# Prompt attention with the values stationary and two heads in column halves, the inverse softmax sums applied later by GpSimd

## The chip, the cores and the metric

The kernel runs on one core of a Trainium2 chip. It is written for the single engines: TensorE (PE, matmuls), VectorE (DVE), ScalarE (ACT), GpSimd (POOL) and SyncE (SP, whose queue issues nearly all DMAs). They run side by side and wait for each other on semaphores. The metric is the device time of one execution in microseconds (us).

## The reference, cut to what matters

One layer of a hybrid decoder is computed for a prompt of 256 positions and for 8 sequences of one new token with 2048 cached positions each: a macaron FFN, a combined projection, latent attention (MLA) beside a convolution branch, a gated merge, and a second FFN. The change lies in the attention of the prompt (16 heads, head width 96 for queries and keys, 64 for values):

```python
s = jnp.einsum('bqhd,bkhd->bhqk', qb, k) * scale
s = jnp.where(k_pos[None, :] <= qp[:, None], s, -jnp.inf)
p = jax.nn.softmax(s, axis=-1)
return jnp.einsum('bhqk,bkhd->bqhd', p, v)
# ... and behind it
a_out = jnp.einsum('bthd,hdo->bto', o, wts['w_attn_out'])
```

## The kernel before, in words

All is written out by hand, one program for each engine, so the order of work on an engine is the order of the code. The stages are: FFN 1, the projections, the prompt heads, the decode rounds (8 sequences of 16 cache pages of 128 positions), the gate stage, the attention output, convolution output and merge products, FFN 2. Products that need more than one pass are three matmuls of fp32r halves (L1894 to L1896, in `product`); the prompt attention, the transposes and the small products are plain fp32 matmuls.

**Prompt heads.** Two query tiles of 128 are kept as rows of scores: the first tile meets 128 keys, the second 256, so a head has 384 score columns. For each head PE makes the scores (L2287, L2288) into one of two PSUM banks. DVE adds the causal mask and puts the result into SBUF as `sS` (L1581), then takes two negated maxima `nm` (L1584, L1585). ACT takes the exponentials into `pS` with their sums `ls` (L1010, L1011). PE turns `pS` with three transposes (`turn_probs`, L2308), ACT copies them to `pTs` (`turned`, L1003), and PE multiplies (`values`): the probabilities are the stationary operand with 128 columns, the values move with 64 columns, three matmuls a head (L2320, L2322, L2323). Every four heads DVE takes reciprocals of the sums (L1593) and scales the result into `otok`, which has query positions on the partitions (`heads_out`, L1596). Scores of head n+2 are issued ahead of the transposes of head n. After the first three score pairs PE also makes one block of the conditioning product (`mod_rows`, L1971). Near the end of the heads PE turns the convolution state of the decode sequences (`turn_state`, L2297, two blocks of eight transposes) and ACT copies it to `stbuf` (L996).

**Decode rounds.** `sequence` goes through 16 pages. For a page PE transposes the cached latent (`turn`, L2342, L2343), ACT and DVE split it into `kTH` (L1026) and `kTL` (L1609), PE makes 18 matmuls with `wqH`, `wqL` (`keys`), ACT squares (L1038), DVE sums (L1614) and puts taps of the convolution between (L1701). At page 10 of the following sequence PE makes the weighted latents (`page_values`, L2367, stationary operands of 32 columns in four strips of the array). At page 6 ACT makes the probabilities (`p_done`) and GpSimd copies one row block of them (L679). SP loads the pages of sequence b+2 when PE has released their slots (`sample_pages`, L418 to L428).

**Gate stage.** Between the gate products PE transposes `otok` back, four transposes for each pair of 128-column blocks (`turn_heads`, L2426), and ACT copies them to `oT` (L1087), from which `oH` and `oL` are split for the attention output product.

Of the kernel before, what the change touches and what calls it, by code (L numbers as in the profile page):

```python
# [87 lines left out]
GATE_BANKS = (2, 6, 4, 6, 4, 6, 4, 6)  # L88

# [49 lines left out]
def decoder_layer(nc, x, out):  # L139
    ctx = ExitStack()  # L140
    with ctx:
# [88 lines left out]
        otok = sb("otok", [P, 2, H, VH], at=o)  # L230
# [18 lines left out]
        sS = sb("sS", [P, 2, 384], at=o + 8192)  # L249
        pS = sb("pS", [P, 2, 384], at=o + 11264)  # L250
        qtokS = qtok[:, 2, 0:H // 4, :]
        pTs = sb("pTs", [P, 2, 384], at=o + 14336)
        zst = sb("zst", [CW - 1 + NB, D], at=X + 14208)
        ctmp = sb("ctmp", [P, 2, T], at=o)
        kTH = sb("kTH", [P, 2, KL], F32R, at=o)
# [5 lines left out]
        oT = sb("oT", [P, KT, T], at=o + 8448)  # L261
# [3 lines left out]
        olrow = sb("olrow", [P, NB // 2, KL], at=o)  # L265
        S = sb("S", [P, 2, NPG + 1, H], at=o + 4096)
# [10 lines left out]
        qrT = sb("qrT", [P, H, NB], at=o); o += 512 + 928  # L277
# [7 lines left out]
        nm = sb("nm", [P, 2, 2], at=o); o += 32  # L285
# [15 lines left out]
        SCORES = [(0, 0), (2, 320)]  # L301

# [57 lines left out]
        ot_ps, ot_sb = sem("ot_ps"), sem("ot_sb")  # L360
# [29 lines left out]
        def _(sp):  # L390
# [226 lines left out]
        def _(pool):  # L617
# [19 lines left out]
            pool.wait_ge(pv_ps, H)  # L637
            nc.gpsimd.memset(Pr[:, :, :, :], 0.0)
            nc.gpsimd.memset(S[:, :, NPG, :], NEG).then_inc(memz, 1)

# [27 lines left out]
            sample_rows(0)  # L668
            for b in range(NB):
# [36 lines left out]
        def _(act):  # L706
# [285 lines left out]
            def state_columns(i):  # L992

                act.wait_ge(st_ps, i + 1)
                for n in range(2):
                    f(stbuf[:, 4 * n:4 * n + 4, 4 * i:4 * i + 4, :].rearrange("p f b t -> p f (b t)"),  # L996
                      PS[:, 6 + n, 0:480].rearrange("p (f c) -> p f c", f=4), ACT.Copy).then_inc(st_sb, 1)

            def turned(hd):
                act.wait_ge(pT_ps, hd + 1)  # L1000
                if hd >= 2:
                    act.wait_ge(pv_ps, hd - 1)
                f(pTs[:, hd % 2, :], PS[:, 2 + hd % 2, 0:384], ACT.Copy).then_inc(pT_sb, 1)  # L1003

            for hd in range(H):
                s = hd % 2
# [4 lines left out]
                f(pS[:, s, 128:384], sS[:, s, 128:384], ACT.Exp, bias=nm[:, s, 1:2], accum_out=ls[:, 1, hd:hd + 1]  # L1011
                  ).then_inc(exp_done, 1)
                if hd >= 1:
                    turned(hd - 1)
                if hd == 15:
                    state_columns(0)
            turned(H - 1)

            def page_hi(pg, n):
                act.wait_ge(kT_ps, pg + 1)
                act.wait_ge(kn_ps, pg + 1)
                if n % 4 == 0:
                    f(krT[:, (n // 4) % 2, :], PS[:, 0, KL:KL + P], ACT.Copy)
                f(kTH[:, n % 2, :], PS[:, 0, 0:KL], ACT.Copy).then_inc(kTH_done, 1)  # L1026
# [25 lines left out]
            def sequence(b, s, first=False, last=False):  # L1052
                for n in range(NPG):
                    pg = NPG * b + n
                    if not (last and n == NPG - 1):
                        page_hi(pg + 1, (n + 1) % NPG)
                    if n == 1 and not first:
                        norm_roots(b - 1, 1 - s)
# [7 lines left out]
            page_hi(0, 0)  # L1066
            state_columns(1)
            act.wait_ge(memz, 6)
# [13 lines left out]
            def heads_turned(i):  # L1082

                act.wait_ge(ot_ps, i + 1)
                if i == 0:
                    act.wait_ge(knsum_done, PAGES + 2)
                f(oT[:, 2 * i:2 * i + 2, 0:SEQ], PS[:, (4, 5, 2, 3)[i], :].rearrange("p (k n) -> p k n", k=2), ACT.Copy  # L1087
                  ).then_inc(ot_sb, 1)

            gate_columns(0)  # L1090
            heads_turned(0)
            heads_turned(1)
            gate_columns(1)
            gate_columns(2)
            heads_turned(2)
            heads_turned(3)
            act.wait_ge(ot_sb, 4)
            act.wait_ge(ysum_done, NB)
            for kt in range(KT):
                f(oH[:, kt, 0:SEQ], oT[:, kt, 0:SEQ], ACT.Copy).then_inc(oh_done, 1)  # L1100
# [5 lines left out]
            act.wait_ge(ot_ps, 5)  # L1106
# [55 lines left out]
        def _(dve):  # L1162
# [412 lines left out]

            def mask_max(hd):
                s = hd % 2
                dve.wait_ge(sc_ps, hd + 1)
                if hd >= 2:
                    dve.wait_ge(exp_done, hd - 1)  # L1580
# [3 lines left out]
                v.tensor_reduce(nm[:, s, 0:1], sS[:, s, 0:128], AX_X, ALU.max, negate=True)  # L1584
# [303 lines left out]
        def _(pe):  # L1888
# [390 lines left out]
            def scores(hd):  # L2279
# [3 lines left out]
                if hd == 1:  # L2283
                    pe.wait_ge(rest_sb, 5)
# [249 lines left out]
```

## Time and profile before

| | us |
|---|---|
| Median of three runs | 1142.21 (1141.67 to 1143.9) |
| The profiled execution, its own time | 1142.67 |
| Its span in the profile | 1140.8 |
| PE busy | 1122.6 (98%) |
| DVE busy | 779.2 (68%) |
| ACT busy | 581.7 (51%) |
| GpSimd busy | 66.9 (6%) |
| Mean granted TensorE clock | 0.997 of full |

The span is the time from the first to the last instruction of the profiled execution; 1.9 us of its own time lie around it. Busy times overlap, so only the engine on which the chain of waits lies sets the end. The chain is given in pieces "start, duration, what"; it counts a matmul from the end of the one before it, so its start times stand some 0.1 to 0.2 us behind those of the timeline for the same instruction. "x2" is the number of instructions in a piece; a plain fp32 matmul shows as two, a transpose as one.

### The profile page before, as it was taken

The numbers are of one execution on the slowest core, as the hardware profiler recorded it, in microseconds if no ns is written. First come the engines' busy times: TensorE is split into PE (matmuls) and PEld (weight loads), VectorE is DVE, ScalarE is ACT, GpSimd is POOL, SyncE is SP. The second block draws the span as 40 slices with busy tenths as digits, with TensorE's granted clock in tenths as the row PEclk, the third lists the DMA queues.
The fourth block names the chain that finished last, engine by engine and source line by source line (L and its number), as shares of the span: only waits on it lengthen the run. The fifth ranks groups of instructions, "written<-read, shape, count | busy, mean of one in ns | idle before, by whom it ended". The sixth has DMA issues, their size and how long they took to land.

```text
span 1140.8 us, 25908 instructions
## 1 busy us (share of the span) xinstructions
PE 1122.6 (98%) x9549; PEld 1087.0 (95%) x9549; DVE 779.2 (68%) x1325; ACT 581.7 (51%) x1153; POOL 66.9 (6%) x136
## 2 busy tenths in 40 slices
PE   5999999999999999999999999999999999999998
PEld 3999999999898999999999999999999999999998
DVE  4655553467777688888888888888756666555543
ACT  3444453346576655554545454554566445444432
POOL 2000000010000100101010110101020010000000
PEclk9899999999999999999999999999999999999999
DMA  9987678947344440021111202031257684555552
GB/s 323 315 296 268 184 254 297 348 162 219 104 140 128 126 140 2 23 62 38 47 52 31 64 20 78 11 91 62 61 153 249 232 267 133 181 183 179 175 186 71
DMA packets 165629, 169.84 MB, mean 149 GB/s; under 512 B 25780, under 2 KB 144071, under 8 KB 165525
## 3 DMA queue, kind: packets, MB, share of 16 engines
q1 hardware_dynamic: 163799, 166.83, 46.3%
q10 hardware_dynamic: 1742, 1.88, 0.5%
q8 instruction: 50, 0.82, 0.3%
q14 instruction: 38, 0.31, 0.1%
HBM read 167.13 MB, written 2.49 MB: 149 GB/s over the span
## 4 chain that ended last, share of the span: by engine, by line
PE 93%; DVE 2%; ACT 1%; DMA 1%; issue 1%; SPq 1%; DVEq 0%; ACTq 0%
PE PS L1894 27%; PE PS L1895 27%; PE PS L1896 27%; PE PS L1971 2%; DMA adaw<-in_w_ada 1%; PE PS L2367 1%; PE PS L2342 1%; PE PS L2343 1%; PE PS L2288 1%; PE PS L2099 1%; PE PS L2338 0%; PE PS L2336 0%; PE PS L2287 0%; PE PS L2308 0%; SPq L451 0%
## 5 line engine op out<-in xcount | busy, mean ns | idle before, releaser
L1172 DVE TENSOR_TENSOR wL<-raw,wH 128x1024 fp32r<-128x1024 f32 (+2 forms) x208 | 247.1, 1194 | 209.1 <-ACT wH L717 206.7
L717 ACT ACTIVATE wH<-raw 128x1024 fp32r<-128x1024 f32 (+2 forms) x208 | 213.1, 1029 | 244.1 <-PE PS L1896 222.3
L1894 PE MATMUL PS<-uH,wH 128*128 128x264 f32 x1024 | 294.5, 288 | 4.1 <-DVE uL L1233 3.7
L1895 PE MATMUL PS<-uL,wH 128*128 128x264 f32 x1024 | 292.3, 285 | 0.0
L1896 PE MATMUL PS<-uH,wL 128*128 128x264 f32 x1024 | 291.9, 285 | 0.0
L1894 PE MATMUL PS<-wqH,kTH 128*128 128x336 f32 (+2 forms) x768 | 256.0, 333 | 0.0
L1896 PE MATMUL PS<-wqH,kTL 128*128 128x336 f32 (+2 forms) x768 | 246.4, 321 | 0.0
L1895 PE MATMUL PS<-wqL,kTH 128*128 128x336 f32 (+2 forms) x768 | 246.3, 321 | 0.0
L1894 PEld LDWEIGHTS PS<-uH,wH 128*128 128x128 f32 x1024 | 194.1, 190 | 7.2 <-issue 6.0
L1895 PEld LDWEIGHTS PS<-uL,wH 128*128 128x128 f32 x1024 | 194.4, 190 | 0.0
L1896 PEld LDWEIGHTS PS<-uH,wL 128*128 128x128 f32 x1024 | 193.9, 189 | 0.0
L1614 DVE TENSOR_REDUCE nsum<-sqb 128x16 f32<-128x1024 f32 x128 | 155.1, 1211 | 1.1 <-ACT sqb L1038 1.1
L1895 PEld LDWEIGHTS PS<-wqL,kTH 128*128 128x128 f32 x768 | 144.8, 189 | 0.0
L1894 PEld LDWEIGHTS PS<-wqH,kTH 128*128 128x128 f32 x768 | 144.6, 188 | 0.0
L1896 PEld LDWEIGHTS PS<-wqH,kTL 128*128 128x128 f32 x768 | 144.3, 188 | 0.0
L1038 ACT ACTIVATE sqb<-PS 128x640 f32<-128x640 f32 (+1 forms) x256 | 138.6, 599 | 0.0
L1035 ACT ACTIVATE S<-PS 128x16 f32<-128x16 f32 x128 | 23.2, 181 | 191.6 <-PE PS L1896 191.5
L1701 DVE SCALAR_TENSOR_TENSOR u<-zbuf,wdw,u (+1 forms) x232 | 113.8, 491 | 8.2 <-DVE u L1701 7.6
L1894 PE MATMUL PS<-aH,wH 128*128 128x264 f32 x352 | 100.8, 286 | 0.0
L1895 PE MATMUL PS<-aL,wH 128*128 128x264 f32 x352 | 100.4, 285 | 0.0
L1896 PE MATMUL PS<-aH,wL 128*128 128x264 f32 x352 | 100.1, 284 | 0.0
L1609 DVE TENSOR_TENSOR kTL<-PS,kTH 128x256 fp32r<-128x256 f32 x128 | 53.9, 421 | 39.9 <-ACT kTH L1026 39.3
(343 smaller groups left out, 1498.7 us busy)
## 6 DMA issues: line engine op xcount, KB each, us to landing
raw<-in_w_ffn_in SPq DMA_DIRECT2D x86, 512.0 KB, 3.6
adaw<-in_w_ada SPq DMA_DIRECT2D x72, 512.0 KB, 6.6
raw<-in_w_ffn_out SPq DMA_DIRECT2D x32, 512.0 KB, 3.5
raw<-in_w_in SPq DMA_DIRECT2D x32, 512.0 KB, 4.6
kv<-in_cache_kv_latent SPq DMA_DIRECT2D x128, 128.0 KB, 2.0
raw<-in_w_ffn_out SPq DMA_DIRECT2D x16, 384.0 KB, 3.1
raw<-in_w_attn_out SPq DMA_DIRECT2D x8, 512.0 KB, 3.9
raw<-in_w_conv_out SPq DMA_DIRECT2D x8, 512.0 KB, 4.1
```

What stands on the lines that cost most here:

```text
L717: f(wH[:, k, 0:width], raw[:, k, 0:width], ACT.Copy).then_inc(w_hi, 1)
L1035: f(S[:, s, n, :], PS[:, b0 + bank, c:c + H], ACT.Copy)
L1038: i_ = f(sqb[:, n % 2, at:at + (k1 - k0) * w].rearrange("p (k w) -> p k w", w=w), PS[:, b0 + k0:b0 + k1, c:c + w], ACT.Square)
L1172: v.tensor_tensor(wL[:, k, 0:width], raw[:, k, 0:width], wH[:, k, 0:width].bitcast(F32), ALU.subtract).then_inc(w_lo, 1)
L1609: v.tensor_tensor(kTL[:, n % 2, :], PS[:, 0, 0:KL], kTH[:, n % 2, :].bitcast(F32), ALU.subtract).then_inc(kTL_done, 1)
L1614: v.tensor_reduce(nsum[:, s, n, :], sqb[:, n % 2, :].rearrange("p (h d) -> p h d", h=H), AX_X, ALU.add).then_inc(knsum_done, 1)
L1701: own.done(v.scalar_tensor_tensor(out=y, in0=z, scalar=w, in1=y, op0=ALU.mult, op1=ALU.add))
L1894: mm(dst, a[0], b[0], start=start, stop=False)
L1895: mm(dst, a[0], b[1], start=False, stop=False)
L1896: return mm(dst, a[1], b[0], start=False, stop=stop)
L1971: i_ = mm(PS[QUAD * g:QUAD * g + NS, bank, 0:P], csil[:, kt, :], w[:, g, :, :], start=(kt == 0), stop=(kt == KT - 1))
L2099: i_ = mm(dst[QUAD * g:QUAD * g + a.shape[1], :], a, parts[g], start=start, stop=stop)
```

## The change

- The scores go to three PSUM banks (`HEAD_BANK`) and stay there: DVE adds only the two diagonal mask blocks (256 columns) in place, takes the maxima from PSUM, and ACT reads PSUM for the exponentials. `sS` is gone, `nm` has four slots, and scores run three heads ahead.
- The values are the stationary operand (64 columns) and the turned probabilities move (256 and 128 columns). Two heads make a pair: one writes partitions 0 to 63, the other 64 to 127 of the same bank. The result has the head's value width on the partitions, as the output product wants it, so `turn_heads` and ACT's copies to `oT` go. DVE copies two pairs at a time, unscaled, to `oTr`.
- The inverse sums `rl` are taken once for all heads, turned by two transposes (`turn_sums`), copied to `rlT`, and spread by 16 SBUF to SBUF transfers on SP's queue, eight into `rlb`, the next eight after the first half has been used. GpSimd multiplies `oTr` by `rlb` in two instructions of 128x1024, behind rounds 0 and 1 of its program (`heads_scaled`).
- `turn_state` is cut into four blocks of four transposes behind heads 5, 7, 9, 11, ACT's copies behind its heads 6, 8, 10, 12; page 0 of the decode rounds is turned behind head 13, page 1 ahead of the last value pair.
- DVE's `latent_out` and ACT's split of `oTr` wait for `o_scaled`. GpSimd clears `Pr` earlier.

```diff
@@ bank choice
+        HEAD_BANK = (0, 7, 1)
+        VALUE_BANK = (4, 5)
@@ SP, ahead of the page loads of sequences 2 to 7
-            sp.wait_ge(st_ps, 2)
+            sp.wait_ge(st_ps, 4)
             sp.dma_start(wuvF[:, :, :], uv).then_inc(in_wuv, 16)
+            sp.wait_ge(rlT_done, 1)
+            sp.wait_ge(pv_ps, PAIRS)
+            for part in range(2):
+                if part == 1:
+                    sp.wait_ge(o_scaled, 1)
+                for j in range(4):
+                    for m in range(2):
+                        hd = 2 * (4 * part + j) + m
+                        sp.dma_start(rlb[VH * m:VH * m + VH, j, :],
+                                     rlT[hd:hd + 1, :].unsqueeze(1).to_broadcast([1, VH, SEQ])).then_inc(in_rl, 16)
@@ GpSimd
+            def heads_scaled(part):
+                pool.wait_ge(in_rl, 128 * (part + 1))
+                z = oTr[:, 4 * part:4 * part + 4, :]
+                g.tensor_tensor(z, z, rlb[:, :, :], ALU.mult).then_inc(o_scaled, 1)
...
+                if b < 2:
+                    if b == 0:
+                        pool.wait_ge(o_sb, 4)
+                    heads_scaled(b)
                 if b < NB - 1:
                     conv_sum(b)
@@ ScalarE, exponentials
-                f(pS[:, s, 0:128], sS[:, s, 0:128], ACT.Exp, bias=nm[:, s, 0:1], accum_out=ls[:, 0, hd:hd + 1])
+                f(pS[:, s, 0:128], PS[:, b, 0:128], ACT.Exp, bias=nm[:, hd % 4, 0:1], accum_out=ls[:, 0, hd:hd + 1])
@@ VectorE
-                v.tensor_tensor(sS[:, s, :], PS[:, s, 0:384], const[:, C_MASK:C_MASK + 384], ALU.add
-                                ).then_inc(masked, 1)
+                z = PS[:, b, :].rearrange("p (a n) -> p a n", n=P)[:, 0:3:2, :]
+                v.tensor_tensor(z, z, tri, ALU.add).then_inc(masked, 1)
...
-                v.tensor_tensor(otok[:, :, hs, :], PS[:, 4 + g % 2, :].rearrange("p (t h d) -> p t h d", t=2, h=4),
-                                rl[:, :, hs].unsqueeze(3).to_broadcast([P, 2, 4, VH]), ALU.mult).then_inc(o_sb, 1)
+                v.tensor_copy(oTr[:, 2 * g:2 * g + 2, :].rearrange("p j n -> p (j n)"),
+                              PS[:, VALUE_BANK[g % 2], :]).then_inc(o_sb, 1)
...
+            dve.wait_ge(exp_done, H)
+            v.reciprocal(rl[:, :, :], ls[:, :, :]).then_inc(rl_done, 1)
+            dve.wait_ge(rl_ps, 1)
+            v.tensor_copy(rlT[:, :], PS[0:H, 6, 0:SEQ]).then_inc(rlT_done, 1)
             heads_out(3)
@@ TensorE
-            def values(hd):
-                b, g, hq = 4 + (hd // 4) % 2, hd // 4, hd % 4
...
-                mm(PS[:, b, c], pTs[:, hd % 2, 0:128], vtok[:, 0, vc], start=True, stop=True)
+            def values(j):
+                g, q = j // 2, j % 2
+                b = VALUE_BANK[g % 2]
+                pe.wait_ge(pT_sb, 2 * j + 2)
...
+                for m in range(2):
+                    hd = 2 * j + m
+                    mm(PS[VH * m:VH * m + VH, b, SEQ * q:SEQ * q + SEQ], vtok[:, 0, VH * hd:VH * hd + VH],
+                       pTs[:, hd % 4, 0:256], start=True, stop=False)
+                for m in range(2):
+                    hd = 2 * j + m
+                    i_ = mm(PS[VH * m:VH * m + VH, b, SEQ * q + 128:SEQ * q + SEQ], vtok[:, 1, VH * hd:VH * hd + VH],
+                            pTs[:, hd % 4, 256:384], start=False, stop=True)
+                i_.then_inc(pv_ps, 1)
...
+            turn_sums()
+            turn(0, 0, 1, 1, 0, True)
+            values(PAIRS - 1)
@@ TensorE, gate stage
-            turn_heads(0, 4)
-            turn_heads(1, 5)
             gate_pair(1)
...
-            turn_heads(2, 2)
-            turn_heads(3, 3)
```

The order of TensorE's instructions in the middle of the heads, before: one head after the other, scores (L2287, L2288), transposes of `pS` (L2308), then three value matmuls.

```order
L2287 MATMUL PS<-kT,qT 128x128
L2288 MATMUL PS<-kT,qT 128x256
L2308 MATMUL PS<-const,pS 128x128 x3
L2320 MATMUL PS<-vtok,pTs 128x64
L2322 MATMUL PS<-vtok,pTs 128x64
L2323 MATMUL PS<-vtok,pTs 128x64
```

The same place after the change, one pair of heads (its lines have moved: L2309 and L2310 are the scores, L2331 the transposes, L2345 and L2349 the values, L2321 a quarter of the convolution state).

```order
L2331 MATMUL PS<-const,pS 128x128 x3
L2309 MATMUL PS<-kT,qT 128x128
L2310 MATMUL PS<-kT,qT 128x256
L2345 MATMUL PS<-pTs,vtok 64x256 x2
L2349 MATMUL PS<-pTs,vtok 64x128 x2
L2331 MATMUL PS<-const,pS 128x128 x3
L2309 MATMUL PS<-kT,qT 128x128
L2310 MATMUL PS<-kT,qT 128x256
L2321 MATMUL PS<-const,strow 128x120 x4
```

Six value matmuls of 64 moving columns in two heads have become four, 64 columns wide in the stationary operand, behind every second head, and the scores stand directly behind the transposes.

The end of the heads on TensorE before, from behind the values of head 14 to the first `keys` matmul (L1894 with `kTH`). L2336 to L2343 turn cache pages 0 and 1, L2297 is the convolution state.

```order
L2336 MATMUL PS<-const,kr_110 128x128
L2342 MATMUL PS<-const,kv_122 128x128
L2343 MATMUL PS<-const,kv_122 128x128
L2320 MATMUL PS<-vtok,pTs 128x64
L2322 MATMUL PS<-vtok,pTs 128x64
L2323 MATMUL PS<-vtok,pTs 128x64
L2297 MATMUL PS<-const,strow 128x120 x8
L2338 MATMUL PS<-qbd,krT 128x64
L2342 MATMUL PS<-const,kv_122 128x128
L2343 MATMUL PS<-const,kv_122 128x128
L1894 MATMUL PS<-wqH,kTH 128x336
```

The same place after the change, from the transposes of head 14 on. L2358 transposes the inverse sums `rl`, L2372 to L2379 turn the pages, L1916 is the first `keys` matmul.

```order
L2331 MATMUL PS<-const,pS 128x128 x3
L2345 MATMUL PS<-pTs,vtok 64x256 x2
L2349 MATMUL PS<-pTs,vtok 64x128 x2
L2331 MATMUL PS<-const,pS 128x128 x3
L2358 MATMUL PS<-const,rl 16x128 x2
L2374 MATMUL PS<-qbd,krT 128x64
L2378 MATMUL PS<-const,kv_122 128x128
L2379 MATMUL PS<-const,kv_122 128x128
L2345 MATMUL PS<-pTs,vtok 64x256 x2
L2349 MATMUL PS<-pTs,vtok 64x128 x2
L1916 MATMUL PS<-wqH,kTH 128x336
```

The state transposes and the page 0 turns are no longer between the last heads and the keys; two transposes of the sums have come in.

## Rows read from the trace of the kernel before

**Rows 1.** The page, part 1: busy time and share of the span by engine.
```profile
PE 1122.6 (98%) x9549; PEld 1087.0 (95%) x9549; DVE 779.2 (68%) x1325; ACT 581.7 (51%) x1153; POOL 66.9 (6%) x136
```

**Rows 2.** Windows, prompt heads: length; busy PE, PEld, DVE, ACT, POOL; clock, DMA share, GB/s.
```profile
359.00:390.50 31.50, 31.35 (x295) 28.66 (x295) 23.16 (x63) 24.75 (x87) 0.86 (x1) 1.00 0.29 75
```

**Rows 3.** Chain, start of the heads (start us, us, what).
```profile
360.00 0.57 DVE sS L1581
...
361.10 0.43 PE PS L2288 x2
361.54 1.86 PE PS L1971 x64
363.40 0.48 PE PS L2308 x3
363.88 0.22 PE PS L2287 x2
```

**Rows 4.** Chain, end of the heads up to the first keys (L1894).
```profile
387.72 0.55 ACT stbuf L996
...
389.58 0.83 PE PS L2297 x8
...
390.81 0.15 PE PS L1894
```

**Rows 5.** Chain, one head in the middle of the stage.
```profile
373.77 0.28 PE PS L2287 x2
374.04 0.43 PE PS L2288 x2
374.48 0.33 PE PS L2308 x3
374.81 0.17 PE PS L2320 x2
374.98 0.22 PE PS L2322 x2
375.20 0.22 PE PS L2323 x2
```

**Rows 6.** Timeline of ScalarE, one head; in brackets idle before it and its releaser.
```profile
367.47 0.40 ACT L1010 ACTIVATE pS<-sS,nm 128x128 f32<-128x128 f32 x1 [0.30 <-DVE nm L1585]
...
368.36 0.47 ACT L1003 ACTIVATE pTs<-PS 128x384 f32<-128x384 f32 x1
```

**Rows 7.** Timeline of VectorE, the mask of one head.
```profile
367.89 0.56 DVE L1581 TENSOR_TENSOR sS<-PS,const 128x384 f32<-128x384 f32 x1 [0.45 <-PE PS L2288]
```

**Rows 8.** Chain, gate stage: transposes of heads, values of the last sequence, gates.
```profile
813.27 0.87 PE PS L2426 x8
...
820.11 1.86 PE PS L2367 x32
821.97 0.32 PE PS L1894
822.29 0.12 PE PS L1895
```

**Rows 9.** Timeline of GpSimd in the decode rounds.
```profile
462.77 0.19 POOL L679 COPY snew<-Pr 8x16 f32<-8x16 f32 x1 [7.96 <-ACT Pr L1050]
...
482.00 1.14 POOL L674 TENSOR_TENSOR krq<-kr 128x512 f32<-128x512 f32 x1 [7.99 <-issue]
```

**Rows 10.** Timeline of VectorE in the decode rounds.
```profile
467.30 0.23 DVE L1605 COPY Srope<-PS 128x64 f32<-128x64 f32 x1 [0.56 <-ACT kTH L1026]
...
481.11 0.48 DVE L1701 SCALAR_TENSOR_TENSOR u<-zbuf,wdw,u  x1
...
482.76 0.67 DVE L1701 SCALAR_TENSOR_TENSOR u<-zbuf,wdw,u  x1
```

**Rows 11.** Timeline of the SP queue in the decode rounds.
```profile
422.67 0.43 SPq L570 DMA_DIRECT2D wuvF<-in_w_uv  x1
476.67 0.34 SPq L425 DMA_DIRECT2D kv<-in_cache_kv_latent  x1
```

More of the change, by code:

```diff
@@ L88 @@
 GATE_BANKS = (2, 6, 4, 6, 4, 6, 4, 6)
+STATE_HEADS = (6, 8, 10, 12)
+PAGE_HEAD = 13
 OUT_KTS = [(0, 4), (4, 8), (8, 12), (12, 16), (16, 19), (19, 22)]
@@ L989, in _, with state_columns, page_hi @@
                 i_.then_inc(zst_done, 1)
[L992 to L997, printed above, removed]
+            def state_columns(k):
+                i, n = k // 2, k % 2
+                act.wait_ge(st_ps, k + 1)
+                f(stbuf[:, 4 * n:4 * n + 4, 4 * i:4 * i + 4, :].rearrange("p f b t -> p f (b t)"),
+                  PS[:, 6, 0:480].rearrange("p (f c) -> p f c", f=4), ACT.Copy).then_inc(st_sb, 1)
             def turned(hd):
                 act.wait_ge(pT_ps, hd + 1)
-                if hd >= 2:
-                    act.wait_ge(pv_ps, hd - 1)
-                f(pTs[:, hd % 2, :], PS[:, 2 + hd % 2, 0:384], ACT.Copy).then_inc(pT_sb, 1)
+                if hd >= 4:
+                    act.wait_ge(pv_ps, (hd - 4) // 2 + 1)
+                f(pTs[:, hd % 4, :], PS[:, 2 + hd % 2, 0:384], ACT.Copy).then_inc(pT_sb, 1)
+            def page_hi(pg, n, bank=0):
+                act.wait_ge(kT_ps, pg + 1)
+                act.wait_ge(kn_ps, pg + 1)
+                if n % 4 == 0:
+                    f(krT[:, (n // 4) % 2, :], PS[:, bank, KL:KL + P], ACT.Copy)
+                f(kTH[:, n % 2, :], PS[:, bank, 0:KL], ACT.Copy).then_inc(kTH_done, 1)
             for hd in range(H):
-                s = hd % 2
+                s, b = hd % 2, HEAD_BANK[hd % 3]
                 act.wait_ge(nmax, hd + 1)
@@ L1056, in sequence @@
                         page_hi(pg + 1, (n + 1) % NPG)
+                    if n == 0 and first:
+                        act.wait_ge(memz, 6)
                     if n == 1 and not first:
@@ L1080, in gate_columns @@
                 f(sig[:, 2 * i:2 * i + 2, :], PS[:, GATE_BANKS[i]:GATE_BANKS[i] + 2, 0:T], ACT.Sigmoid).then_inc(g_free, 1)
[L1082 to L1097, printed above, removed]
+            for i in range(3):
+                gate_columns(i)
+            act.wait_ge(o_scaled, 2)
             act.wait_ge(ysum_done, NB)
             for kt in range(KT):
-                f(oH[:, kt, 0:SEQ], oT[:, kt, 0:SEQ], ACT.Copy).then_inc(oh_done, 1)
+                f(oH[:, kt, 0:SEQ], oTr[:, kt, :], ACT.Copy).then_inc(oh_done, 1)
             gate_columns(3)
@@ L1608, in page_lo @@
                     denominators(b - 1)
-                v.tensor_tensor(kTL[:, n % 2, :], PS[:, 0, 0:KL], kTH[:, n % 2, :].bitcast(F32), ALU.subtract
+                v.tensor_tensor(kTL[:, n % 2, :], PS[:, bank, 0:KL], kTH[:, n % 2, :].bitcast(F32), ALU.subtract
                                 ).then_inc(kTL_done, 1)
@@ L2327, in denominator, with turn @@
                 mm(PS[:, 0, 448:448 + H], ones[:, :], lsum[:, s, :], start=True, stop=True).then_inc(den_ps, 1)
-            def turn(use, s, n, pg, b, first):
+            def turn(use, s, n, pg, b, first, bank=0):
                 if n % 4 == 0:
@@ L2375, in sequence @@
                     if n + 1 < NPG:
-                        turn(use, s, n + 1, pg + 1, b, first)
+                        if not (first and n == 0):
+                            turn(use, s, n + 1, pg + 1, b, first)
                     elif not last:
@@ L2388, in _ @@
             pe.sem_inc(pg_rel, 8)
-            scores(0)
-            scores(1)
+            for hd in range(3):
+                scores(hd)
             for hd in range(H):
-                if hd + 2 < H:
-                    scores(hd + 2)
                 if hd == 0:
@@ L2397, in _ @@
                 turn_probs(hd)
[L2398 to L2406 removed]
+                if hd + 3 < H:
+                    scores(hd + 3)
+                if hd >= 2 and hd % 2 == 0:
+                    values(hd // 2 - 1)
+                if hd + 1 in STATE_HEADS:
+                    turn_state(STATE_HEADS.index(hd + 1))
+                if hd == PAGE_HEAD:
+                    pe.wait_ge(st_sb, 4)
+                    turn(0, 0, 0, 0, 0, True, 6)
+            turn_sums()
+            turn(0, 0, 1, 1, 0, True)
+            values(PAIRS - 1)
             pe.wait_ge(o_sb, 3)
[L2410 removed]
             sequence(0, 0, 0, first=True)
@@ L2419, in gate_pair @@
                 pair(Q_GATE + i // 2, [(0, 2 * m), (0, 2 * m + 1)], [(0, 4), (4, 8)], GATE_BANKS[i], (uH, uL), KT)
-            def turn_heads(i, bank):
-                for kt in range(2 * i, 2 * i + 2):
-                    for t in range(2):
-                        c = SEQ * (kt % 2) + P * t
-                        i_ = tr(PS[:, bank, c:c + P],
-                                otok[:, t, 2 * kt:2 * kt + 2, :].rearrange("p h d -> p (h d)"), ident)
-                i_.then_inc(ot_ps, 1)
             pe.wait_ge(knsq_done, PAGES + 1)
```

136 lines of the change are left out of this document (61 added, 75 removed).

## The prediction

> **What bounds the kernel now.** I read the share of busy time first: PE is busy for 98% of the span [rows 1], so time is won only where PE has less to do or waits less. In the window of the prompt heads PE is busy for 31.35 of 31.5 us at the full granted clock, while DVE has 23.16 us and ACT 24.75 us of work in it [rows 2]. The chain of waits then shows where inside the stage anything but PE ends the time: at its start, where the third scores wait for DVE's mask at 360.00, and at its end, where ACT's copy of the convolution state and PE's transposes of it stand on the chain [rows 3, 4]. In between all is PE, head after head. The reader is to see one head in the middle: scores 0.28 + 0.43, transposes 0.33, values 0.17 + 0.22 + 0.22, together 1.65 us [rows 5]. ACT has about 1.36 us of work in that step, since it idles for 0.30 [rows 6], and DVE about 1.2 us, since it idles for 0.45 [rows 7]. The gate stage is PE alone as well; the transposes of heads stand on the chain with 0.87 us for eight [rows 8].
>
> **Scores.** Directly behind transposes the first scores matmul costs 0.22 us [rows 3], behind values 0.28 [rows 5]. In the new order scores always stand behind transposes, so a head's scores cost 0.22 + 0.43 = 0.65. The third scores no longer wait for a mask but use a third bank: the first scores end about 0.1 before DVE's mask starts at 360.00, so at 359.9, two more take 2 x 0.65 and end at 361.2, and `mod_rows` (1.86) ends at 363.06 instead of 363.40 [rows 3].
>
> **Values.** No row shows stationary operands of 64 columns. From below: 384 moving columns for two heads side by side. The nearest row is `page_values`: 32 instructions of 256 columns in four strips take 1.86 us [rows 8]; four strips at a time that is 16 matmuls in four groups, 1.86 / 4 = 0.465 us for 256 columns. For 384 columns I get 0.70. From above: if the two halves ran one after the other, a pair would take twice that, 1.40. The matmul behind a block in strips takes 0.32 instead of 0.12, and the transposes behind `mod_rows` 0.48 instead of 0.33 [rows 8, 3, 5]: 0.15 to 0.20 us on leaving a block in strips. I take 0.70 + 0.20 = 0.90 for a pair, since four strips side by side are in the trace and two should be the easier case; ends 0.70 and 1.60. Before, a pair took 2 x 0.61 = 1.22.
>
> The Trainium skill (TensorEngine Tiling (Array Packing), Key Properties) says that tiles work in parallel, but that a change of the tiling mode drains TensorE. That speaks against this change, which goes in and out of column tiles eight times; the 0.15 to 0.20 us above is what this trace shows of it, and the page gives no figure. Without the drain the sum below would be 1.6 us better, by the row it is as given.
>
> **The sum on PE in the heads.** From 363.06, in the chain's way of counting: 16 transposes (the first 0.48, 15 x 0.33) 5.43; 13 scores x 0.65 = 8.45; 7 value pairs x 0.90 = 6.30; the state in four blocks, 2 x 0.83 = 1.66 [rows 4]; page 0 turned, three transposes, 0.33. Together 22.17, so PE alone would be through the last transposes at 385.2. ACT: a head costs 1.36 [rows 6], and it now also copies the state (4 x about 0.5 [rows 4]) and page 0 (two copies of 384 columns together; I estimate 0.55 from 0.47 for 384 in one) before its last exponentials. Until head 12 PE has more to do (1.43 a head on average, and 0.42 for each state block). From head 13 on no scores are left: PE has 0.33 + 0.33 + 0.33 + 0.90 = 1.9 us up to the last transposes, ACT 2 x 1.36 + 0.55 = 3.3. ACT comes into this with a lead of about half of the difference, so PE waits some 0.7 (between 0 and 1.4). The last transposes end at 385.9. Then the sums' two transposes 0.22, page 1 turned 0.41 (389.58 + 0.83 to 390.81 is 0.40 [rows 4]), and the last pair 0.90: the keys begin at 387.4. They began at 390.81 [rows 4]. **Won in the heads: 3.4 us.** DVE's reciprocal and the copy of turned sums stand beside this work. DVE's mask shrinks from 384 to 256 columns, its maxima and ACT's exponentials read PSUM; I cost these at the old durations, hidden by PE, with 0.1 to 0.2 us a head to spare on ACT. If ACT's part grew by 0.1 a head, only the end would feel it.
>
> **What stands behind the wait at the end.** PE's `turn_sums` waits for DVE's reciprocal, and behind it are page 1, the last values and all keys. The reciprocal needs only the last exponentials, as PE's transposes do, so it is done while these run. The last values need ACT's last copy (0.47 [rows 6]), covered by 0.22 + 0.41.
>
> **Gate stage.** Two blocks of `turn_heads` go: 2 x 0.87 = **1.74 us** off the chain [rows 8]. ACT loses four copies that were off the chain. What PE waits for there (gate chunks, means) comes from ACT and DVE in answer to PE's own progress, so it moves with it.
>
> **Decode rounds.** GpSimd multiplies 1024 columns twice. `krq` is 512 columns in 1.14 us [rows 9], so about 2.3 us each, starting after the copy at 462.77 and again one sequence later. GpSimd has no other work there. SP comes to the new transfers after its loads at 423.1 and issues eight (about 0.43 each, 3.5 us) into an empty queue. Before the second eight it waits for GpSimd's first multiply, at about 465.1, and behind that wait are the page loads of sequence 2. These begin only at 476.67 because PE releases the slots no earlier [rows 11]. The second eight are issued by 469, so 7 us are to spare. Cost: nothing.
>
> **Together** 3.4 + 1.74 = 5.1 us. Against the profiled execution's own 1142.67 that is 1137.5; that execution stands 0.46 above the median 1142.21, so by the median it is 1137.1. I predict 1137.3.
>
> **Rivals.**
> - *Leaving the halves is cheaper than 0.20.* At 0.70 a pair PE gains 8 x 0.2 = 1.6 more, of which ACT's end eats about a third: 1136.2. For it: 0.20 was seen on full fp32r matmuls, transposes showed 0.15. Chance 0.14.
> - *The two halves do not run side by side.* 1.60 a pair, 8 x 0.70 = 5.6 us more, which takes back the gate stage too: 1142.8. Against it: `mod_rows` packs 64 instructions of 128 columns into 1.86 us, 0.03 each, where a transpose of 128 columns takes 0.11 [rows 3, 5]. Chance 0.08.
> - *The multiplies of GpSimd hold up DVE.* While `krq` ran (482.00 to 483.14) a DVE tap took 0.67 instead of 0.48 [rows 9, 10]. If DVE stood for a whole multiply of 2.3 us, less the 0.56 it idles per page anyway [rows 10], and PE's keys waited for it, it would cost 2 x 1.7 = 3.4: 1140.7. Chance 0.09. The Trainium skill (SBUF — State Buffer, on the port pair that VectorE and GpSimd share) says that a VectorE instruction with two SBUF inputs is blocked for the whole of a GpSimd instruction that reads SBUF. The trace shows 0.19 us of delay for it, less than a full block; by the page the rival's price holds.
> - *Every change of half drains PE (slower).* A pair has three changes inside. With 0.20 each and no overlap it is 1.40 + 4 x 0.20 = 2.2, and 8 x 1.3 = 10.4 us more than forecast: 1147.7. It decides from 1.54 us a pair on (0.90 + 5.1 / 8). The 0.03 us of `mod_rows`, where the strip changes all the time, speaks against it. Chance 0.05.
> - *The order of the heads does not fit* (PE waits for ACT or DVE in every pair, as the end suggests): 1 to 3 us lost, 1139 to 1140.5. Chance 0.08.
>
> **How the numbers follow.** The forecast has the remaining 0.56. Likely it lies at 1137.3, its own unknowns (0 to 1.4 of waiting, 0.1 a pair) spread it from 1136.2 to 1138.8. To hold 8 in 10 the range takes in the cheaper exit and most of the two middle rivals: 1135.6 to 1140.2. 0.2% (2.3 us) is about what a measurement of this kernel can tell from no change; faster by more than that is below 1139.9. Forecast, cheaper exit, and about two thirds of the middle rivals are there: 0.82. Within 0.2%: halves in sequence (two thirds) and the rest of the middle rivals: 0.11. Slower: 0.07.
>
> **What the changed profile would show.** Right: L2345 and L2349 of a pair together about 0.7 us on the chain, the transposes behind them 0.45 to 0.55; steps of about 1.4 us a head without idle PE; first keys near 387.4; no transposes of heads in the gate stage, the gates shorter by 1.74; the two multiplies about 2.3 us each with no wait of PE beside them. Wrong: 1.4 us for a pair's values, PE waiting for ACT's exponentials in every head, a wait of PE for `kTL` beside a multiply, or page loads of sequence 2 later than PE's release.

## The result and the profile after

| us | before | after |
|---|---|---|
| Median of six runs | 1141.94 (1141.33 to 1144.4) | 1148.34 (1146.23 to 1150.99) |
| Profiled execution | 1142.67 | 1146.43 |
| Its span | 1140.8 | 1144.6 |
| Mean granted TensorE clock | 0.997 | 0.994 |

The changed kernel is slower: the ratio is 1.0049, interval 1.0038 to 1.0060. Forecast were 1137.3 and a range of 1135.6 to 1140.2. The profiled execution of after is one of its faster ones, so the traces differ by 3.8 us of span where the medians differ by 6.4. The readings below explain the 3.8.

The page, part 1, of the changed kernel (busy time and share by engine), which answers to [rows 1]:

```profile
PE 1119.9 (98%) x9503; PEld 1079.4 (94%) x9503; DVE 777.6 (68%) x1323; ACT 578.1 (51%) x1149; POOL 73.1 (6%) x138
```

PE has 2.7 us less to do and the span is 3.8 us longer. So PE waits more, by about 6.5 us. In part 4 of the page (the chain that ended last, share by engine) the queue of SP, SPq, has risen to 4% from 1% before. "issue" is time for which the profile shows no wait:

```profile
PE 88%; SPq 4%; issue 2%; DVE 2%; ACT 2%; DMA 1%; POOL 0%; DVEq 0%; ACTq 0%; POOLq 0%
```

To find the place I cut both spans at instructions that both kernels have: the first scores, the first keys matmul, and the first matmul of `page_values` of each decode sequence. The chain gives the first two, the timeline of PE the others.

```
                              before    after    after - before
start of the heads            359.03    359.38   +0.35
heads, to the first keys       31.78     28.68   -3.10
to page_values, sequence 0     84.34     84.55   +0.21
sequence 0 to sequence 1       52.36     60.43   +8.07
sequence 1 to the last in the
 gate stage                   292.53    291.72   -0.81
from there to the end         320.76    319.84   -0.92
```

The heads and the gate stage (two transposed blocks, -0.81 and -0.92) give what they were to give. All of it and more is lost in one round. There PE waits once; the waits of PE in the changed kernel (us in total, times, longest), first and sixth row of the view:

```profile
PE PS L2372 <- DMA kr<-in_cache_k_rope: 6.0, 1, 6.0
...
PE PS L2378 <- DVE kTL L1625: 0.9, 3, 0.4
```

The chain of the changed kernel through that wait (start us, us, what):

```profile
460.22 0.19 POOL snew L707
460.47 6.96 issue
467.43 2.39 POOL oTr L695
469.84 0.46 SPq L589
470.34 0.60 SPq L589
470.98 0.60 SPq L589
471.62 1.62 SPq L589
473.28 2.38 SPq L589
475.71 2.39 SPq L589
478.14 1.88 SPq L589
480.07 2.20 SPq L589
482.59 2.21 SPq L428
...
491.34 0.34 SPq L435
491.86 1.81 DMA kr<-in_cache_k_rope
493.80 0.47 PE PS L2372
```

Read it backwards. PE waits for a page of sequence 2. SP loaded it late because it came out of the second eight transfers (L589) only at 482.3. They began at 469.84, behind GpSimd's multiply, and took 12.4 us to issue. The multiply began 7 us after GpSimd's copy at 460.22, with nothing between them that the profile shows. The forecast had SP free at 468.6, so it is 13.7 late: 4.7 because the multiply ended at 469.8 and not at 465.1, 9.0 because eight issues took 12.4 and not 3.5.

The windows of the changed kernel around it (length; busy PE, PEld, DVE, ACT, POOL; clock, DMA share, GB/s):

```profile
474.00:478.00 4.00, 4.00 (x37) 3.58 (x30) 3.23 (x8) 0.66 (x4) 0.00 (x0) 1.00 0.82 27
...
490.00:492.00 2.00, 0.00 (x0) 0.00 (x0) 0.00 (x0) 0.00 (x0) 0.00 (x0) 0.50 0.28 74
...
494.00:496.00 2.00, 2.00 (x8) 2.00 (x8) 0.68 (x2) 0.55 (x2) 0.00 (x0) 0.50 0.35 95
496.00:498.00 2.00, 2.00 (x13) 2.00 (x13) 1.66 (x3) 0.00 (x0) 0.00 (x0) 0.87 0.23 60
```

Two things stand here. While the transfers run, the DMA engines are busy for 82% of the time and move only 27 GB/s. And PE's idle time costs more than its length: it idles from 487.8, the granted clock is at 0.50 (the 1.2 GHz level) by 490, and it is at full again only after 496. In between matmuls of the keys take 0.32 us on the chain, where 0.15 to 0.17 is usual. That is about 2.5 us of work at half speed, 1.2 us lost. So the 8.07 are 6.0 to 6.3 of idle PE, 1.2 of half clock, and 0.4 to 0.6 of waits for `kTL`.

### The profile page after: what moved, and what is told of

It reads as the page before. It is cut to its first block, busy times and chain, and to the rows that moved or that the text cites. A ratio compares the mean times of both kernels' runs of the same rounds, so it can differ in the third digit from the quotient of the medians.

```text
span 1144.6 us, 25822 instructions
## 1 busy us (share of the span) xinstructions
PE 1119.9 (98%) x9503; PEld 1079.4 (94%) x9503; DVE 777.6 (68%) x1323; ACT 578.1 (51%) x1149; POOL 73.1 (6%) x138
## 4 chain that ended last, share of the span: by engine, by line
PE 88%; SPq 4%; issue 2%; DVE 2%; ACT 2%; DMA 1%; POOL 0%; DVEq 0%; ACTq 0%; POOLq 0%
PE PS L1916 26%; PE PS L1917 26%; PE PS L1918 26%; PE PS L1993 2%; SPq L461 2%; PE PS L2378 1%; PE PS L2403 1%; DMA raw<-in_w_ffn_in 1%; PE PS L2379 1%; SPq L589 1%; PE PS L2310 1%; PE PS L2121 1%; PE PS L2331 1%; DVE wL L1190 0%; PE PS L2374 0%
## 5 line engine op out<-in xcount | busy, mean ns | idle before, releaser
L1916 PE MATMUL PS<-uH,wH 128*128 128x264 f32 x1024 | 294.4, 288 | 4.4 <-DVE uL L1251 3.8
L1916 PE MATMUL PS<-wqH,kTH 128*128 128x336 f32 (+2 forms) x768 | 256.3, 334 | 0.0
L1916 PEld LDWEIGHTS PS<-uH,wH 128*128 128x128 f32 x1024 | 194.0, 189 | 7.9 <-issue 6.1
L1916 PEld LDWEIGHTS PS<-wqH,kTH 128*128 128x128 f32 x768 | 144.9, 189 | 0.2 <-issue 0.2
L1723 DVE SCALAR_TENSOR_TENSOR u<-zbuf,wdw,u (+1 forms) x232 | 116.1, 500 | 8.2 <-DVE u L1723 7.6
L1916 PE MATMUL PS<-aH,wH 128*128 128x264 f32 x352 | 100.7, 286 | 0.0
```

Of the source, the lines that this page charges most:

```text
L1723: own.done(v.scalar_tensor_tensor(out=y, in0=z, scalar=w, in1=y, op0=ALU.mult, op1=ALU.add))
L1916: mm(dst, a[0], b[0], start=start, stop=False)
```

## The experiments

Theory A: SP comes back to the page loads of sequence 2 too late, and that is the whole loss. The rivals: the loss comes from GpSimd's multiply (it holds DVE, which is late with `kTL`), or it sits in the new heads.

**late_part: the page loads ahead of the second eight.** The order of SP's queue alone is changed.

```diff
-            for part in range(2):
-                if part == 1:
-                    sp.wait_ge(o_scaled, 1)
...
-            with sp.Fori(1, 4) as i:
+            spread(0)
+            sample_pages(1, 0)
+            sp.wait_ge(o_scaled, 1)
+            spread(1)
+            sample_pages(1, 1)
+            with sp.Fori(2, 4) as i:
```

> The changed kernel with one thing moved: SP issues the second eight transfers of inverse sums (and waits for GpSimd's first multiply) behind the page loads of sequence 2 instead of ahead of them. Theory A (the whole loss is the SP queue: 12 us of issue between the end of the first multiply and the page loads, then a 6 us wait of PE and its slow clock behind it): PE's wait ahead of sequence 2 is gone, the distance between the first weighted latents of sequences 0 and 1 is 52.4 us again (60.4 in the changed kernel, 52.36 before), and the time is that of before less 2.6 (heads) and 1.8 (gate stage): 1137.6, ratio 0.996. Theory B (the multiplies and transfers also cost through the shared port or the DMA engines): a good part of the 8 us stays, time above 1140. Theory C (values in column halves lose later what the heads gain): no better than before.

Measured: 1138.63 (1138.38 to 1140.45, five runs), before on the same chip 1142.01, ratio 0.9965 (0.9952 to 0.9979). The waits of PE hold no `kr` or `kv` any more; from `page_values` of sequence 0 to that of sequence 1 it takes 53.08. One change of order turns 0.5% slower into 0.35% faster, and every transfer and multiply is still there. This version is faster than both kernels.

**early_mult: the first multiply ahead of all rounds, the second where the first was.** SP would get its `o_scaled` early.

```diff
+            pool.wait_ge(o_sb, 4)
+            heads_scaled(0)
             for b in range(NB):
                 pool.wait_ge(kTH_done, NPG * b + 14)
...
-                if b < 2:
-                    if b == 0:
-                        pool.wait_ge(o_sb, 4)
-                    heads_scaled(b)
+                if b == 0:
+                    heads_scaled(1)
```

> The changed kernel with GpSimd's multiplies moved instead: the first stands behind the first block of sample rows, ahead of round 0, the second where the first stood. SP's order is unchanged. Theory A: the wait of SP for the first multiply now ends near 441 instead of 470, the second eight transfers are issued by about 455, the page loads of sequence 2 start when PE releases the slots, and the time is 1137.6 as well. The first multiply now stands in sequence 0, where VectorE has the most work: if a VectorE instruction stands still for the whole multiply (2.4 us) and PE's keys wait for it, 1 to 2 us are lost here against the kernel with only the transfers moved. If the 7 us that GpSimd idles ahead of its multiply belongs to the multiply, it shows here too; if it belongs to the reduction over partitions ahead of it, the first multiply has none.

Measured: 1149.82 (1149.48 to 1150.84, five runs), ratio 1.0062 (1.0048 to 1.0076). A miss: it moved the stall instead of lifting it. GpSimd's timeline in early_mult (in brackets idle before it and its releaser):

```profile
442.71 2.34 POOL L695 TENSOR_TENSOR oTr<-oTr,rlb 128x1024 f32<-128x1024 f32 x1 [51.08 <-DMA rlb<-rlT]
445.01 1.04 POOL L704 TENSOR_TENSOR krq<-kr 128x512 f32<-128x512 f32 x1
```

Behind it DVE, in the same kernel:

```profile
446.08 0.69 DVE L1672 TENSOR_REDUCE ssr<-krq 128x16 f32<-128x512 f32 x1 [10.65 <-POOL krq L704]
```

And PE, first row of its waits:

```profile
PE PS L2374 <- DVE kTL L1625: 9.5, 1, 9.5
```

The first eight transfers land only at 442.7, and `krq` of sequence 0 is queued behind the multiply that waits for them. DVE waits for `krq`, PE for DVE's `kTL`. I had asked only who waits for the multiply, not what stands behind it. There is no wait for `kr` in this run, so SP was in time, as theory A has it; the loss is another one. The run also tells where the gap of 7 us belongs: this first multiply starts when its transfers have landed, the second, behind the reduction across partitions, has 7.3 us of idle time ahead of it. The gap belongs to the reduction, not to the multiply.

**no_second: the second eight transfers are left out, the wait for `o_scaled` stays.** The second half of the heads is scaled by the first half's sums.

```diff
                         hd = 2 * (4 * part + j) + m
+                        if part == 1:
+                            continue
                         sp.dma_start(rlb[VH * m:VH * m + VH, j, :],
...
-                pool.wait_ge(in_rl, 128 * (part + 1))
+                pool.wait_ge(in_rl, 128)
```

> The changed kernel without the second eight transfers: the second multiply uses the inverse sums of the first half again (heads 8 to 15 are scaled by the sums of heads 0 to 7). The wait of SP for the first multiply stays ahead of the page loads. Theory A1 (the issue of eight transfers, 12 us, is the cost): SP is free at 470, before PE releases the slots at about 473; no wait of PE, 1137.6. Theory A2 (the wait itself is the cost): the page loads are late as before and the time stays near 1146 to 1148.

Measured: 1139.37 (eight runs, seven from 1137.34 to 1140.19 and one of 1562.13 with a mean granted clock of 0.657, which has no trace and stays unexplained), ratio 0.9970 (0.9959 to 0.9980) without that one. In the changed kernel PE needed the pages at 487.8 and they came 11.5 us after SP was free (482.3 to 493.8), so SP must be free by about 476.3. That is an estimate on the early side, since two steps of SP in these 11.5 us took 2.2 and 1.4 us, where 0.3 is usual. With the late multiply alone it would be free by 469.8 + 3.5 = 473.3. Neither the 7 us gap nor the wait is enough to lose anything; the 12.4 us of issue are what passes the limit.

**before_plus: the kernel before, with 16 such transfers added on SP's queue**, eight ahead of the decode rounds' loads and eight once GpSimd is past the first step of its second block of sample rows. They copy rows of the constant table, and nobody uses them; `latent_out` on DVE waits for their landing.

```diff
+            sp.wait_ge(pv_ps, H)
+            for part in range(2):
+                if part == 1:
+                    sp.wait_ge(in_rl, 128)
+                    sp.wait_ge(own_pool, 9)
+                for j in range(4):
+                    for m in range(2):
+                        sp.dma_start(rlb[VH * m:VH * m + VH, j, :],
+                                     const[VH + j:VH + j + 1, C_ROPE:C_ROPE + SEQ].unsqueeze(1).to_broadcast([1, VH, SEQ])
+                                     ).then_inc(in_rl, 16)
```

> The kernel before with only the transfers added: eight transfers of one row to 64 partitions each (of a constant table, into memory that nothing reads) behind the last heads, and eight more when GpSimd is through the first step of its second block of sample rows (about 471), ahead of the page loads of sequence 2. Nothing is multiplied. Theory A: the second eight keep SP until about 483, the loads come some 4 us too late for PE (PE is 2.6 us later in this kernel than in the changed one), and with the slow clock behind the wait the kernel is 5 to 6 us slower than before: 1147.5. Theory C (the loss comes with the values in halves or the multiplies): no change from before.

Measured: 1152.01 (1150.99 to 1153.11, four runs), ratio 1.0081 (1.0065 to 1.0096). The old heads and no multiply at all, and the loss appears: from `page_values` of sequence 0 to that of sequence 1 it takes 9.83 us more. It is larger than I expected. SP issues from 471.04 to 484.15 here, 1.9 later than in the changed kernel, PE waits 7.0, and the half clock lasts longer. Windows of before_plus:

```profile
498.00:500.00 2.00, 2.00 (x8) 2.00 (x8) 2.00 (x4) 0.00 (x0) 0.00 (x0) 0.50 0.25 74
500.00:502.00 2.00, 2.00 (x9) 2.00 (x8) 0.29 (x1) 0.00 (x0) 0.00 (x0) 0.50 0.32 78
502.00:504.00 2.00, 2.00 (x15) 2.00 (x15) 0.03 (x1) 1.44 (x4) 0.00 (x0) 0.94 0.27 74
```

PE works again from about 496.4 and has the full clock only at 502: 5.6 us at half, 2.8 lost, where the changed kernel lost 1.2.

The next four ask what is left of the multiplies and why an issue takes so long.

**mid_mult: the first multiply behind `krq` of sequence 0**, the second where the first was.

```diff
                 nc.gpsimd.tensor_tensor(krq[:, :, :], kr, kr, ALU.mult).then_inc(kr_sq, 1)
+                if b == 0:
+                    pool.wait_ge(o_sb, 4)
+                    heads_scaled(0)
```

> The changed kernel with only GpSimd's order moved: the first multiply stands directly behind the squares of the rope keys of sequence 0 (so nothing of VectorE waits behind it on GpSimd, as it did in the run with the early multiply), the second where the first stood. The first eight transfers land near 443, the multiply ends near 445, the second eight are issued by 458, SP is free long before PE releases the slots. Theory A (only SP's lateness costs): PE has no wait ahead of sequence 2, time as with the late second half, 1138.6. Theory B (something of the multiplies' place matters as well): clearly off from 1138.6 either way.

Measured: 1139.92 (1137.6 to 1140.89, seven runs), before 1142.69 on this chip, ratio 0.9969 (0.9957 to 0.9980). The first multiply stands at 441.55, behind `krq` and ahead of the reduction, and the last of SP's 16 issues begins at 455.5 (480.1 in the changed kernel). This is what early_mult was meant to be, and it differs from it by one position in GpSimd's queue.

**no_scale: no transfers and no multiplies**, so the heads stay without their inverse sums.

```diff
-                pool.wait_ge(in_rl, 128 * (part + 1))
-                z = oTr[:, 4 * part:4 * part + 4, :]
-                g.tensor_tensor(z, z, rlb[:, :, :], ALU.mult).then_inc(o_scaled, 1)
+                pool.sem_inc(o_scaled, 1)
```

The 16 `dma_start` on SP and the wait for `o_scaled` among them go as well.

> The changed kernel without the sixteen transfers and without both multiplies: the attention output of the prompt stays unscaled by the inverse sums. It shows what the heads and the gate stage give alone. Theory A (the spread and the multiplies are free once SP's order fits): same as with the late second half, 1138.6 within 0.5. Theory B (they cost 1 us more through VectorE, which stands while GpSimd multiplies): 1137.0 to 1137.8, and no instruction of VectorE's taps longer than 0.7 near 469 and 522.

Measured: 1138.58 (1138.19 to 1139.98, five runs), ratio 0.9964 (0.9950 to 0.9977). That is late_part's ratio: once SP's order fits, spreading and multiplying cost nothing that shows in the medians. Round 0 takes 52.36, exactly as before, against 53.08 in late_part, so late_part's trace shows 0.7 us there; where they come from is told below (the multiply and DVE). And it is what the heads and the gate stage alone are worth: 0.36%, or 4.1 us.

**thin: 16 columns of each row are spread, not 256.** GpSimd sets the other columns of `rlb` to one beforehand and SP waits for that, so most positions are not scaled.

```diff
-                        sp.dma_start(rlb[VH * m:VH * m + VH, j, :],
-                                     rlT[hd:hd + 1, :].unsqueeze(1).to_broadcast([1, VH, SEQ])).then_inc(in_rl, 16)
+                        sp.dma_start(rlb[VH * m:VH * m + VH, j, 0:16],
+                                     rlT[hd:hd + 1, 0:16].unsqueeze(1).to_broadcast([1, VH, 16])).then_inc(in_rl, 16)
```

> The changed kernel with transfers of 16 columns instead of 256: as many transfers and rows of 64 bytes instead of 1024, one row still going to 64 partitions (the other columns are scaled by one). Theory D1 (the time that a transfer holds SP is a price for each row of it): a transfer takes SP 1.8 us as before (median), and the wait of PE ahead of sequence 2 stays at 6 us. Theory D2 (it is back pressure by bytes): a transfer takes 0.5 us, the wait is gone, 1138.6.

**many_rows: the same 64 rows of 1 KB with the same destinations, but read from 64 partitions** of the constant table (the heads are scaled by numbers of that table).

```diff
-                                     rlT[hd:hd + 1, :].unsqueeze(1).to_broadcast([1, VH, SEQ])).then_inc(in_rl, 16)
+                                     const[VH:2 * VH, C_ROPE:C_ROPE + SEQ]).then_inc(in_rl, 16)
```

> The changed kernel with transfers of the same size and destination, but each from 64 partitions of a table instead of 64 times from one partition (the attention output is scaled by numbers of the table). Theory D3 (reading one partition 64 times is what is slow): a transfer takes SP 0.35 to 0.5 us, lands in 2 to 3 us as the cache pages do, and the wait of PE is gone, 1138.6. Theory D1 or D2 (rows or bytes): 1.8 us each and the wait stays.

Measured: thin 1139.24 (1137.46 to 1140.26, four runs), ratio 0.9963 (0.9949 to 0.9978); many_rows 1139.63 (1139.24 to 1140.84, five runs), ratio 0.9971 (0.9959 to 0.9984). What tells more is the view of the one line L589 in three kernels: the 16 issues (ns min/median/max), and the time to landing. The changed kernel:

```profile
L589 SPq DMA_DIRECT2D rlb<-rlT x16: 464/1751/3296, 421.8 to 480.1; - x16
...
DMA to landing us min/median/max: 4.5/8.9/10.2
```

thin:

```profile
L589 SPq DMA_DIRECT2D rlb<-rlT x16: 464/597/603, 422.3 to 474.4; - x16
...
DMA to landing us min/median/max: 1.9/2.0/4.6
```

many_rows:

```profile
L589 SPq DMA_DIRECT2D rlb<-const x16: 462/597/623, 423.7 to 474.3; - x16
...
DMA to landing us min/median/max: 1.9/2.3/5.0
```

All three write 64 partitions a transfer. It is not the number of rows (thin has 64 too, at 0.60 us an issue), and not the bytes written (many_rows writes as many as the changed kernel, at 0.60 and 2.3). Only 64 KB read out of one SBUF partition are slow: 1.75 us of SP's time, up to 3.3, and 8.9 us to land in a row of eight (the quickest 4.5). before_plus reads one row of the constant table in this way and has 2.08 and 10.1, so it is not the tensor that is read. Whether the partition counts or the address that is read 64 times, no run tells apart. The pace of the issues in the chain fits a queue that fills. The first three of the second eight cost 0.46, 0.60 and 0.60, and from the fifth on SP is let go at the pace of the transfers, 1.9 to 2.4. That it is a full queue that holds SP is my reading; no run varied the depth.

## Why the prediction was wrong

**The step that failed** is the one under "Decode rounds": "GpSimd has no other work there", "issues eight (about 0.43 each, 3.5 us)", "The second eight are issued by 469, so 7 us are to spare. Cost: nothing." Both terms of it were off.
- The multiply was to start right behind the copy at 462.77. The trace before already held the gap that I did not read. Timeline of GpSimd in the kernel before, the instruction behind that copy's neighbour:

```profile
462.91 0.40 POOL L662 COPY ysum<-u 128x264 f32<-128x264 f32 x1
470.57 0.66 POOL L647 TENSOR_TENSOR ztmp<-stbuf,wdw 128x240 f32<-128x240 f32 x1 [7.27 <-issue]
```

  In the next three sequences the same gap is 6.7 to 7.1 us. It stands between the copies and the first operation on two tensors behind them. In the changed kernel the multiply is that operation. Cost to SP: 4.7 us, inside the 7 to spare.
- The issue price came from a load of `wuvF` [rows 11], one transfer into an idle queue. I had no row of a transfer within SBUF, let alone one that reads one partition 64 times, and gave no upper end for it. Cost: 9.0 us more, and that passes the limit of about 476.3 (no_second, thin and many_rows each remove all or most of it, and each is faster than before).

A late SP stood in the text only as a sign under "Wrong". As a rival it would have needed a price, and the price would have shown that the margin of 7 us hung on one guessed duration.

**The heads: mechanism right, size close.** Chain of the changed kernel, scores, then values of a pair (L2345, L2349) and the transposes behind them:

```profile
366.08 0.43 PE PS L2310 x2
366.52 0.58 PE PS L2345 x4
367.10 0.22 PE PS L2349 x4
367.32 0.48 PE PS L2331 x3
```

A pair is 0.58 + 0.22 = 0.80, and the transposes behind it take 0.15 more than 0.33: 0.95 where I took 0.90. Scores cost 0.65 as forecast, a state block 0.41 for 0.415. `mod_rows` ends at 363.41; less the 0.35 by which all began later that is the forecast 363.06. At the end ACT stands on the chain for 4 us, and by the chain's count it costs PE the 0.7 us that were forecast:

```profile
382.13 0.03 issue
...
385.05 0.51 ACT pS L1049 x2
385.56 0.46 ACT pS L1050 x2
386.02 0.04 issue
386.06 0.55 PE PS L2331 x3
386.61 0.23 PE PS L2358 x2
...
387.23 0.61 PE PS L2345 x4
387.84 0.22 PE PS L2349 x4
388.06 0.35 PE PS L1916
```

The last transposes were forecast to end at 385.9, 386.25 with the late start, and end at 386.61: seven pairs at 0.05. From there to the keys it is 1.45, and the first keys matmul takes 0.35 instead of 0.15, so 1.65 against 1.53. Won: 2.9 us by this count for 3.4 forecast. (That "in between all is PE" was read too shortly from the trace before: there the chain already leaves PE for DVE and ACT from 382.80 to 388.70. The sum does not rest on it.)

**The gate stage** gave 0.81 + 0.92 = 1.73 for 1.74.

**The rivals.** The two halves one after the other (1.40 a pair and more) and a drain at every change of half (2.2) are refuted by 0.80. (The price of the first, 5.6 us on 1137.3, is 1142.9 and not 1142.8.) The exit costs 0.15 on transposes and 0.20 on full matmuls, so the cheaper exit is half right. The Trainium skill (TensorEngine Tiling (Array Packing), Key Properties) says that a change of mode drains TensorE; these 0.15 to 0.20 us fit it and are all that the trace shows of it. The order of the heads fits: no wait of PE for ACT or DVE in the pairs.

**The multiply and DVE** was under-weighed. I set 0.19 us of delay at `krq` against a full block. DVE's timeline in the changed kernel, while the multiply ran from 467.43 to 469.81:

```profile
468.08 0.41 DVE L1625 TENSOR_TENSOR kTL<-PS,kTH 128x256 fp32r<-128x256 f32 x1
468.41 1.69 DVE L1723 SCALAR_TENSOR_TENSOR u<-zbuf,wdw,u  x1
470.02 1.21 DVE L1630 TENSOR_REDUCE nsum<-sqb 128x16 f32<-128x1024 f32 x1
```

A tap of 0.48 lasted 1.69, to 0.29 us behind the multiply's end; in late_part it is 2.00, in thin 2.32 and in many_rows 1.41, and each ends 0.28 to 0.29 behind its multiply. So DVE stood until GpSimd was done. The tap of 0.67 beside `krq` that the prediction read as less than a full block [rows 9, 10] was one too: it started 0.38 ahead of `krq`'s end and ended 0.29 behind it. The Trainium skill (SBUF — State Buffer, Who interferes with whom) says that a VectorE instruction with two SBUF inputs contends with a GpSimd instruction that reads SBUF, and that the lock on the ports they share is exclusive. The trace agrees here. The `kTL` ahead of the tap, which reads PSUM and SBUF, took its usual 0.41.

What the rival got wrong is the price and its place. In the stretch with the first multiply PE loses nothing: in its timeline it takes from the first keys matmul to `page_values` of sequence 0 84.59 us before, 84.61 in no_scale, which has no multiply, and 84.62 in late_part. But DVE comes out of the multiply late, and seven us behind `page_values` GpSimd makes the next `krq`. Three lines of late_part's timelines, in order of time:

```profile
480.14 1.20 POOL L707 TENSOR_TENSOR krq<-kr 128x512 f32<-128x512 f32 x1 [5.21 <-issue]
480.62 1.00 DVE L1728 SCALAR_TENSOR_TENSOR u<-zbuf,wdw,u  x1 [0.18 <-DVE u L1728]
482.27 0.33 PE L2383 MATMUL PS<-const,kv 128*128 128x128 f32 x1 [0.19 <-DVE kTL L1630]
```

The tap starts behind the start of `krq`, stands until 0.28 behind its end, and the `kTL` behind it comes late for PE. It is this order that decides. Counted from `page_values` of sequence 0, `krq` starts at 6.84 to 6.85 in each of five traces. The tap starts ahead of it at 6.61 (before and no_scale) or 6.74 (many_rows), takes 0.48 to 0.49, and the round takes 52.36, 52.36 and 52.37; it starts behind it at 6.91 (mid_mult) or 7.32 (late_part), and the round takes 52.92 and 53.08. Thin has 53.58, and many_rows pays one round later (53.86 for 52.69 before). So a multiply costs PE nothing while it runs, and nothing or up to 1.2 us afterwards, not 1.7, and the medians show nothing of it.

**What stays open.** The medians differ by 2.6 us more than the two profiled executions. The longest run of the changed kernel has the lowest mean clock (1150.99 at 0.992, the shortest, 1146.23, at 0.994), which fits a longer stretch at half clock behind the idle time, as in before_plus; but the run of 1149.1 has 0.994 as well, so that is not shown. There is no profile of such a run of the changed kernel. And the forecast gain of 5.1 us shows as 3.4 to 4.1 in the medians of late_part and no_scale: 0.5 of the difference is in the heads, the rest lies within the intervals.

## What to carry to other kernels

Before adding transfers to a queue, find the next ones behind them, the latest time at which the queue must be free for these, and bound the issue time of the new ones from above; a hold of SP in one round was worth more than all that PE saved. A queue in order has two neighbours to ask about: who waits for the moved instruction, and what is queued behind it and waits with it (early_mult and mid_mult differ in just the second). To spread one row to many partitions, avoid reading it many times out of one SBUF partition, or put such transfers where nothing urgent is behind them.

## What the runs showed of the hardware

- A transfer within SBUF of 64 rows of 1 KB that all come from one partition, eight issued in a row, takes 8.9 us to land and holds the issuing queue for 1.75 us (medians); from 64 partitions it is 2.3 and 0.60. The DMA engines show as 82% busy at 27 GB/s meanwhile.
- Behind a reduction across partitions GpSimd still makes its copies when ACT releases them, but its next operation on two tensors starts some 7 us late (6.7 to 7.7 behind the last copy in the first two rounds of all ten traces), with nothing in the profile. Without the reduction ahead there is no such gap, neither behind an operation on two tensors (early_mult, `krq` 445.01 behind the multiply) nor behind a copy (changed kernel, `ysum` copied at 469.77, the next operation on two tensors at 470.34). The Trainium skill (GPSIMD Engine Reference, Instruction dispatch) speaks of about 6 us for loading code at the first call of a newly loaded GpSimd kernel, without an instruction in the profile. The size is near that, but here the gap comes back in every round; no run here shows that it is code loading.
- 6 to 7 us of idle PE cost 1.2 to 2.8 us more, since the granted clock stays at the 1.2 GHz level for 2.5 us (changed kernel) to 5.6 us (before_plus) of the work behind it.
- A VectorE tap (`u<-zbuf,wdw,u`, usually 0.48 us) that starts while GpSimd multiplies or makes `krq` ends 0.27 to 0.29 us behind GpSimd's operation, whatever was left of it (0.67 to 2.32 us). Taps that started 0.11 and 0.24 us ahead of `krq` (many_rows, before) took 0.49; one that started 0.03 ahead (many_rows, 532.19) stood as well.
- Two fp32 matmuls side by side in column halves, 64 columns each: the couple with 256 moving columns takes 0.58 us, with 128 it takes 0.22, and leaving the halves 0.15 to 0.20.
